# A two-block transformer on one core: gate banks, order of the mixers' last gates, and a split value product

## What is computed

```python
uv, c_q, c_kv, k_rope, z, xbc, dt_raw, gates = jnp.split(h @ w_in[l], IN_OFFSETS, axis=-1)
y_a = gmlp_mixer(uv, ...)                    # spatial gating
y_b = mla_mixer(c_q, c_kv, k_rope, ...)      # causal attention, 8 heads of 96
y_c = ssd_mixer(z, xbc, dt_raw, ...)         # state-space scan, 2 chunks of 128
g = jax.nn.sigmoid(gates).reshape(bsz, s, N_BRANCH, D_MODEL)
merged = (g[:, :, 0] * (y_a @ w_branch[l, 0])
          + g[:, :, 1] * (y_b @ w_branch[l, 1])
          + g[:, :, 2] * (y_c @ w_branch[l, 2]))
x = x + merged @ w_out[l]
```

## Time and profile before

| | |
|---|---|
| median of 3 runs | 3313.93 us (3313.74 to 3315.62) |
| profiled execution | 3314.97 us, its span 3313.2 us |
| PE busy | 3198.2 us, 97% |
| PEld busy | 2727.8 us, 82% |
| DVE busy | 1944.1 us, 59% |
| ACT busy | 1294.7 us, 39% |
| mean granted clock of TensorE | 0.987 of 2.4 GHz |
| chain that ended last | PE 89%, DVE 5%, issue 2%, ACT 2% |
| fp32 value product, L953 | 96 records, 41.8 us busy |

### The profile page before, as it was taken

How to read it: one execution, slowest core, us unless ns; L and a number is a source line. 1 busy time by engine, 2 the same in 40 slices (tenths; PEclk the granted TensorE clock), 3 DMA queues, 4 the chain that set the end, 5 groups by cost and what they waited for, 6 DMA issues and landing times.

```text
span 3313.2 us, 42938 instructions
## 1 busy us (share of the span) xinstructions
PE 3198.2 (97%) x17262; PEld 2727.8 (82%) x17262; DVE 1944.1 (59%) x2685; ACT 1294.7 (39%) x1785; POOL 103.3 (3%) x144
## 2 busy tenths in 40 slices
PE   8999889999998899999999999999999999999898
PEld 8988779899887799788877777778887888887797
DVE  6868568867686577674243344577334753345655
ACT  5446444444464454422223322232223222245543
POOL 1000000000000000000000000000000000022000
PEclk9999999999998999999999999999999999999999
DMA  7754347767553376553323222145333533253354
GB/s 242 243 188 166 112 139 258 248 210 235 177 171 122 127 237 224 174 179 109 114 90 101 77 89 77 64 163 168 99 111 108 188 130 105 99 134 89 98 183 153
DMA packets 334911, 496.96 MB, mean 150 GB/s; under 512 B 11042, under 2 KB 221884, under 8 KB 334716
## 3 DMA queue, kind: packets, MB, share of 16 engines
q1 hardware_dynamic: 330652, 483.46, 43.9%
q0 software_dynamic: 4064, 10.77, 1.5%
HBM read 493.09 MB, written 1.10 MB: 149 GB/s over the span
## 4 chain that ended last, share of the span: by engine, by line
PE 89%; DVE 5%; issue 2%; ACT 2%; POOL 1%; DMA 0%; DVEq 0%; POOLq 0%; ACTq 0%
PE bank L531 28%; PE bank L532 28%; PE bank L533 28%; DVE wlo L1550 1%; PE bank L953 1%; ACT whi L1090 1%; PE bank L661 1%; PE bank L544 1%; PE bank L676 0%; PE bank L938 0%; POOL small L2357 0%; POOL small L2362 0%; DVE bank L2294 0%; DVE small L2290 0%; ACT npr L1498 0%
## 5 line engine op out<-in xcount | busy, mean ns | idle before, releaser
L1550 DVE TENSOR_TENSOR wlo<-raw,whi 128x1024 fp32r<-128x1024 f32 (+1 forms) x780 | 933.9, 1211 | 995.6 <-ACT whi L1090 993.7
L1090 ACT ACTIVATE whi<-raw 128x1024 fp32r<-128x1024 f32 (+1 forms) x780 | 813.5, 1049 | 1189.8 <-PE bank L533 1186.9
L531 PE MATMUL bank<-xTh,whi 128*128 128x256 f32 (+1 forms) x3200 | 1045.5, 327 | 6.1 <-DVE xTl L1606 6.0
L533 PE MATMUL bank<-xTh,wlo 128*128 128x256 f32 (+1 forms) x3200 | 1039.4, 325 | 0.0
L532 PE MATMUL bank<-xTl,whi 128*128 128x256 f32 (+1 forms) x3200 | 1039.3, 325 | 0.0
L531 PEld LDWEIGHTS bank<-xTh,whi 128*128 128x128 f32 x3200 | 610.6, 191 | 68.7 <-issue 19.7
L533 PEld LDWEIGHTS bank<-xTh,wlo 128*128 128x128 f32 x3200 | 610.3, 191 | 49.1
L532 PEld LDWEIGHTS bank<-xTl,whi 128*128 128x128 f32 x3200 | 610.7, 191 | 48.3 <-issue 0.5
L531 PE MATMUL bank<-whi,hh 128*128 128x512 f32 x968 | 377.6, 390 | 0.0
L533 PE MATMUL bank<-whi,hl 128*128 128x512 f32 x968 | 376.7, 389 | 0.0
L532 PE MATMUL bank<-wlo,hh 128*128 128x512 f32 x968 | 376.6, 389 | 0.0
(11 more groups left out here) (337 smaller groups left out, 2318.4 us busy)
## 6 DMA issues: line engine op xcount, KB each, us to landing
raw<-in_ffn_w_in_dram SPq DMA_DIRECT2D x176, 1024.0 KB, 5.4
raw<-in_ffn_w_out_dram SPq DMA_DIRECT2D x80, 1024.0 KB, 5.0
mraw<-in_w_mod_dram SPq DMA_DIRECT2D x72, 1024.0 KB, 5.1
raw<-in_w_in_dram SPq DMA_DIRECT2D x44, 1024.0 KB, 5.1
raw<-in_ret_w_in_dram SPq DMA_DIRECT2D x24, 1024.0 KB, 5.1
raw<-in_w_branch_dram SPq DMA_DIRECT2D x12, 1024.0 KB, 5.0
raw<-in_nat_w_qkv_dram SPq DMA_DIRECT2D x12, 1024.0 KB, 5.1
raw<-in_ffn_w_out_dram SPq DMA_DIRECT2D x16, 512.0 KB, 3.6
```

The lines of the kernel that those rows point to most:

```text
L531: pe.matmul(ps, lh, rh, start=start, stop=False, skip_group_check=True)
L533: return pe.matmul(ps, ll, rh, start=False, stop=stop, skip_group_check=True)
L1090: nc.scalar.activation(hi, src, ACT.Copy).then_inc(*e.inc("hi", key, part))
L1550: nc.vector.tensor_tensor(lo, src, hi.bitcast(F32), ALU.subtract).then_inc(*e.inc("lo", key, part))
```

## The change

What it does, in four parts.

1. The rings: `SHORT` becomes banks 0 to 3, `LONG` 4 to 7. The units of the mixers of block one that came from `ALL` behind the first state of the scan now come from one of the smaller rings: branches, the turned outputs b and c, the second chunk's products and the output projection from `SHORT`, its sums from banks 6, 7, 4 and 5, the turned merged rows from `LONG`.
2. The order of TensorE and of the slabs: gate (2,1) is one slab half before and one behind `branch(1,0)`, with the turned outputs between its parts; then branches (2,0), (1,1), the first merged rows turned, branch (2,1). The other engines follow.
3. ScalarE and VectorE: the sigmoids of gate (1,1), the fourth projection, stand behind the last exponential in step 8 of the attention; in a step, turned pieces are copied before the split and the exponentials come behind it on ScalarE, and the maxima before it on VectorE. `heads_scaled` is divided into the sum and the scaling with other work between, `heads_rotated(1)` goes from before `turned_y(a)` to before `merge(0,0)`, `scan_decays(1)` before `scan_rows(0)`.
4. The value product of the retention: values and weighted scores are split into `rvh`, `rvl`, `rah` and `ral` and multiplied by `mm3`. The gate's rows `gbm` move to the place of `WX` and `wtmp`, and are loaded once head 3's weighted scores stand.

```diff
-SHORT, LONG = (0, 1, 2, 3, 4), (5, 6, 7)
-ALL, SCORES, TURNED, VALUES, UPPER = tuple(range(8)), (0, 1, 2, 3), (4, 5), (6, 7), (4, 5, 6, 7)
+SHORT, LONG = (0, 1, 2, 3), (4, 5, 6, 7)
+ALL, TURNED, VALUES = tuple(range(8)), (4, 5), (6, 7)
...
         gate(0, 1)
-        branch(0)
+        branch(0, 0)
+        branch(0, 1)
         gate(1, 0)
         gate(1, 1)
         gate(2, 0)
-        branch(1)
-        gate(2, 1)
-        branch(2)
+        c = GATES + 2 * D + 512
+        s.add((("g", l, 2, 1), 0), rows(m, 0, 4, c, 512), 4, 512)
+        branch(1, 0)
+        s.add((("g", l, 2, 1), 1), rows(m, 4, 4, c, 512), 4, 512)
+        branch(2, 0)
+        branch(1, 1)
+        branch(2, 1)
         for half in range(2):
             for n in range(2):
...
@@ -866,28 +879,32 @@
                 branch(0, 0, ytT[1])
                 scan_sums(1)
                 branch(0, 1, ytT[1])
-                gate(1, 0, lambda part: (head_turned(0) if part == 1 else attention(part - 2) if part > 1 else None))
+                gate(1, 0, -2)
                 scan_inside(1)
                 pe.wait_ge(*e.at("st", l))
-                ps = new("yo", l)
+                ps = new("yo", l, ring=SHORT)
...
-                gate(2, 0, lambda part: attention(6 + part))
-                turn_y(("b", l), yb, 4, 256, ("yb", l))
-                turn_y(("c", l), z, 4, 256, ("yc", l))
+                gate(1, 1, 2)
+                gate(2, 0, 6)
+                g21 = gate_banks(2, 1)
+                gate_part(2, 1, g21, 0)
+                turn_y(("b", l), yb, 4, 256, ("yb", l), SHORT)
+                gate_part(2, 1, g21, 1)
+                turn_y(("c", l), z, 4, 256, ("yc", l), SHORT)
                 pe.wait_ge(*e.at("yT", ("b", l), 1))
-                for n in range(2):
-                    branch(1, n, ytT[1])
-                gate(2, 1)
+                branch(1, 0, ytT[1])
+                gate_part(2, 1, g21, 2)
+                gate_part(2, 1, g21, 3)
                 pe.wait_ge(*e.at("yT", ("c", l), 3))
                 branch(2, 0, ytT[0])
+                branch(1, 1, ytT[1])
 
                 def merged_turned(n):
                     for u in range(2 * n, 2 * n + 2):
-                        ps = new("ty", ("m", l), u)
+                        ps = new("ty", ("m", l), u, ring=LONG)
                         for j in range(2):
                             for t in range(2):
                                 pe.wait_ge(*e.at("mg", l, n, t))
...
-                rows_by(("b", l, 2, 1), ("bp", l, 2, 1), b2, *ytT[0], 0, 4, (0,))
                 merged_turned(0)
-                rows_by(("b", l, 2, 1), ("bp", l, 2, 1), b2, *ytT[0], 2, 4, (1,))
+                branch(2, 1, ytT[0])
                 pe.wait_ge(*e.at("yT", ("m", l), 1))
                 wo = {}
                 for n in range(2):
-                    wo[n] = {t: new("wop", l, n, t) for t in range(2)}
+                    wo[n] = {t: new("wop", l, n, t, ring=SHORT) for t in range(2)}
                     rows_by((("wo", l, n), 0), ("wop", l, n), wo[n], *xT[256], 0, 8)
                     if n == 0:
                         merged_turned(1)
...
                     m.then_inc(*e.inc("rap", h, 1 + jt))
 
             def retained(h):
-                pe.wait_ge(*e.at("ra", h, 2))
-                pe.wait_ge(*e.at("rv", h, 3))
+                pe.wait_ge(*e.at("ral", h, 2))
+                pe.wait_ge(*e.at("rvl", h, 3))
                 for t in range(4):
                     ps = new("rop", h, t)
                     if t < 2:
-                        pairs = [(ra[:, 0, 256 * jt + t * P:256 * jt + (t + 1) * P], jt) for jt in range(2)]
-                        pairs += [(ra[:, 1 + jt, t * P:(t + 1) * P], 2 + jt) for jt in range(2)]
+                        pairs = [(0, 256 * jt, jt) for jt in range(2)] + [(1 + jt, 0, 2 + jt) for jt in range(2)]
                     else:
-                        pairs = [(ra[:, 1 + jt, t * P:(t + 1) * P], 2 + jt) for jt in range(2)]
-                    for i, (a, j) in enumerate(pairs):
-                        m = pe.matmul(ps[:, :], a, rv[:, j, :], start=i == 0, stop=i == len(pairs) - 1)
+                        pairs = [(1 + jt, 0, 2 + jt) for jt in range(2)]
+                    for i, (u, c, j) in enumerate(pairs):
+                        cols_of = slice(c + t * P, c + (t + 1) * P)
+                        m = mm3(ps[:, :], rah[:, u, cols_of], ral[:, u, cols_of], rvh[:, j, :], rvl[:, j, :],
+                                i == 0, i == len(pairs) - 1)
                     m.then_inc(*e.inc("rop", h, t))
 
...
@@ -1334,7 +1349,8 @@
                         if h >= 2:
                             act.wait_ge(*e.at("op", l, h - 2))
                         A(pT[h % 2][:, :], unit("ptp", l, h)[:, 0:384], ACT.Copy).then_inc(*e.inc("pT", l, h, frees=("ptp", l, h)))
-                    if i < HEADS:
+                    after(key, part)
+                    if 0 <= i < HEADS:
                         h = i
                         act.wait_ge(*e.at("nmax", l, h))
                         if h >= 2:
@@ -1346,9 +1362,9 @@
                               bias=small[:, o + 3:o + 4], accum_out=small[:, o + 5:o + 6])
                         m.then_inc(*e.inc("pr", l, h, frees=("sc", l, h)))
 
-                ahead(until, (("g", l, 0, 0), 0))
...
@@ -1359,26 +1375,38 @@
                 for n in range(2):
                     ahead(until, ("b", l, 0, n))
                 scan_exps(1)
-                gate(1, 0, lambda part: (head_turned(0) if part == 1 else attention(part - 2) if part > 1 else None))
+                gate(1, 0, -2)
                 sigmoids(1, 0)
-                gate(1, 1, lambda part: attention(2 + part))
-                sigmoids(1, 1)
-                gate(2, 0, lambda part: attention(6 + part))
+                gate(1, 1, 2)
+                for part in range(4):
+                    attention(6 + part, (("g", l, 2, 0), part // 2), part % 2)
+                    if part == 2:
+                        sigmoids(1, 1)
                 sigmoids(2, 0)
+                after((("g", l, 2, 1), 0), 0)
                 turned_y(("b", l), 4, 256, ytT[1][0])
+                after((("g", l, 2, 1), 0), 1)
                 turned_y(("c", l), 4, 256, ytT[0][0], lambda c: col(0, SSN + 4 * l + c))
-                for n in range(2):
-                    ahead(until, ("b", l, 1, n))
-                gate(2, 1)
+                for part in range(2):
+                    after(("b", l, 1, 0), part)
+                for part in range(2):
+                    after((("g", l, 2, 1), 1), part)
                 sigmoids(2, 1)
-                for n in range(2):
-                    ahead(until, ("b", l, 2, n))
+                for part in range(2):
+                    after(("b", l, 2, 0), part)
+                for part in range(2):
+                    after(("b", l, 1, 1), part)
+
+                def merged_turned(n):
                     for u in range(2 * n, 2 * n + 2):
                         act.wait_ge(*e.at("ty", ("m", l), u))
                         A(xT[256][0][:, 2 * u:2 * u + 2, :], unit("ty", ("m", l), u)[:, :]
                           .rearrange("p (j t) -> p j t", t=256), ACT.Copy).then_inc(*e.inc("yh", ("m", l), u))
-                    if n == 0:
-                        after(("b", l, 2, 1), 1)
+
+                merged_turned(0)
+                for part in range(2):
+                    after(("b", l, 2, 1), part)
+                merged_turned(1)
                 for n in range(2):
                     after((("wo", l, n), 0), 1)
                 after((("wo", l, 0), 1), 0)
...
+                    act.wait_ge(*e.at("ra", h, u))
+                    A(rah[:, u, :], ra[:, u, :], ACT.Copy).then_inc(*e.inc("rah", h, u))
                 if h == 1:
                     first_rows(0)
                 if h:
...
@@ -1997,6 +2034,8 @@
                         V.tensor_reduce(small[:, o:o + 1], ps[:, 0:P], AX, ALU.max)
                         link(V.tensor_reduce(small[:, o + 1:o + 2], ps[:, 256:512], AX, ALU.max))
                         TS(small[:, o + 2:o + 4], small[:, o:o + 2], -QK ** -0.5, None, ALU.mult).then_inc(*e.inc("nmax", l, h))
+                    if i < HEADS + 1:
+                        after(key, part)
                     if 2 <= i < HEADS + 2:
                         h = i - 2
                         o = 112 + 8 * (h % 2)
@@ -2010,10 +2049,12 @@
                         o = 112 + 8 * (h % 2)
...
@@ -2041,50 +2082,54 @@
                 ahead(until, ("kv", l))
                 dve.wait_ge(*e.at("kvp", l, 1, 1))
                 scan_decays(0)
-                ahead(until, (("uv", l, 1), 0))
+                after((("uv", l, 1), 0), 0)
+                heads_summed(0)
+                after((("uv", l, 1), 0), 1)
                 heads_scaled(0)
                 ahead(until, (("uv", l, 1), 1))
-                heads_rotated(0)
+                heads_rotated(0, lambda: after((("uv", l, 1), 1), 1))
```

(45 more changed lines are left out.)

110 lines of the change are left out of this document (62 added, 48 removed).

## The result

The changed kernel takes 3236.92 us, median of 4 runs (3233.21 to 3237.75), the kernel before 3314.53 us in the same comparison: a ratio of 0.9763, 95% interval 0.9747 to 0.9780. That is 77.6 us less. I had forecast 69.1 us less and 3245 us, with 3238 us as the low end: the time lies 1.1 us under the range. In the profiled executions the span went from 3313.2 to 3235.0 us, by 78.2 us.

The account below looks back on a forecast made before the run. TensorE bounds the kernel; its idle and slow-clock time in block one's mixers can go. Mixers 64.6 - 5.0 = 59.6, value product 8.5, key-copy wait 1.0: 69.1 us off 3314.97, median 3245 us; own range 3239 to 3255, eight-in-ten 3238 to 3264.

Parts of the forecast that it names:

- the charge: Both mixers of block one: 2.5 us a mixer held back for late banks and a tight place missing with clock drop.
- The clock term: Both mixers of block one: time lost at TensorE's lower clock comes back, about 9.8 us a mixer, 19.6 us.
- (1): Ahead of the gates, VectorE works while waiting for GpSimd's roots; TensorE's waits for low weight halves go, 1.2 us a mixer.
- (2): At `branch(0,0)`, rotating the second tile's heads later removes the 3.1 us wait; gate (1,0) finds its banks 0.6 us late.
- (3): Four gate banks remove waits at diagonal product (5.7, 4.5 us), gate (2,0) (4.7), attention turns (3.0); last gate waits 0.2 us.
- (4): ScalarE's two fewer table loads of 1.28 us a mixer are on no path: 0; without cover 1.3 us each.
- (5): Attention step on four banks instead of five: cost 0, ScalarE's exponentials having 1.2 us to spare.
- (6): Mixer tail: split last gate and interleaved branches remove waits of 1.7, 1.9 and 2.5 us; tightest merges spare 0.4, 0.3.
- A: VectorE replaces the waits as bound, gate (1,0) and merges late: 12 to 20 us more, say 3260 us; chance 0.22.
- B: Mixers' gates are not freed, sigmoids stay in the path: only 21 us gained, 3293 us; chance 0.05.
- C: Many short waits keep TensorE at 1.2 GHz from `branch(0,0)` to the last merge: 3365 us; chance 0.04.
- D: Both mixers: none of the 2.5 us a mixer held back is lost, 3240 us; chance 0.04.

## Why the prediction was wrong, and where it was right

**The idle time** was right: 43.3 us against 43.4 us, and even the charge in its place, 0.5 us at gate (1,0) in both mixers where I had 0.6 us. The mechanism (gates that hold banks, VectorE late, merges too close) is what the profile shows.

**The clock term, with the charge in it, is the step that failed:** 16.2 us forecast, 23.9 us less busy time measured. The 7.7 us are three things. First, 3.4 us of charge: a tight place in each mixer that would miss and draw a fall of the clock. No such fall came; the changed mixers have one, at the start of the first, and the kernel before has it too. Second, the price of the slowed stretches: I had 9.8 us a mixer, 19.6 us, from pairs of equal work of which one is shown; the stretches themselves give 21.0 us, 1.4 us more. Two waits, of 4.46 and 4.69 us, were followed in the second mixer by 6.8 us at 1.2 GHz each, and two in the first, of 5.71 and 2.99 us; the one pair of which I showed the rows lies in a stretch of 3.4 us. Third, a term that the sum did not have: 2.9 us of busy time that went with the waits and is no clock. The trace of before could have given the second: busy time in the stretches with a granted clock of 0.50, halved. The Trainium skill (TensorE: Matmul & The Clock Gate, HAM oscillation — how this bites in real kernels) reckons so, extra time as half of the time at 1.2 GHz. The two mixers agree: by that rule the clock gave back 21.0 us, the 19 waits fewer at 0.16 us each make 3.0 us, and the 24.0 us together stand against 23.9 us measured. A rougher way, the granted clock times the window, gives 0.05 x 279.90 + 0.04 x 279.24 = 25 us before and 0.01 x 246.87 = 2.5 us after, and counts idle time at the low clock as well.

**The range** let the low end go to 3238 us, "no charge and a little more clock". With its own bound, 12 us a mixer and no charge, it would have reached 3245 - 5.0 - 4.4 = 3235.6 us; it would have been right by luck in part, as that bound counts idle time and the 2.9 us are none of the clock's. Its other side was wide for a rival that did not come (VectorE the bound, 0.22).

**Outside the mixers** I had 9.5 us, it was 11.0 us. Between the releases at 1731.87 and 2164.33 us before, 1663.48 and 2087.29 us after, the stage of the value product took 432.46 and 423.81 us: 8.65 us against my 8.5 us. The wait for the key copy is gone (1.0 us). The other 1.3 us have no cause that I can name: they are within the 6 us by which the same work differed between kernels.

**By parts.** (1) and (2): I gave the rotation 3.1 us and the roots 1.2 us a mixer. With the rotation alone undone 0.4 and 0.6 us of the wait are back, with the roots as well 1.6 and 1.7 us, with ScalarE's scan exponentials too 3.0 and 3.2 us: three edits share what I gave to one, so the attribution was wrong though the sum was right. The roots' own 1.2 us a mixer were right (2.4 us in both). (3): the gates' waits went, and with the banks alone. The late sigmoids, on which I had the last gate depend, and (4), the two loads fewer, are worth nothing: right for the loads; the last gate doesn't need the late place. (5): cost 0, right, but my 1.2 us to spare held for the old order of the step; in the new one even 3.65 us more of ScalarE (two loads and the sigmoids) fit. (6): the waits in my list are 1.7 + 2.5 us in the first mixer and 1.7 + 1.9 + 2.5 us in the second, 10.3 us, to which comes the clock behind them; the tail is worth 13.4 to 14.7 us. Both tight merges held. (What I expected of the run with the old tail counts the 1.9 us in both mixers, which is one too many.)

**Rivals.** A did not come: VectorE had room at the turned columns (1.49 us idle) and the gate waited 0.5 us. B did not: the run with banks alone excludes it. C did not: the changed mixers have 8 waits and a granted clock of 0.99 and 1.00, and nine short waits in a feed-forward left the clock alone; whether a denser row would bring C about is open. D, no charge at all, was the nearest, at 3240 us: of the 4.1 us that it lacked against the profiled executions the clock's price makes 1.4 us, the busy time of the waits 2.9 us and all outside the mixers 1.5 us, less 1.7 us of waits that stayed.

## What to carry to other kernels

Price the clock by the stretches in which it is granted at 0.50, half of TensorE's busy time in them, and not by a pair of rows. Busy time over equal instruction counts holds more than the clock: each wait adds a little to it. Where the sum names a bound, the range has to reach it. Judge an edit of a few microseconds between marks that both kernels share: the total moved by up to 6 us for the same work. Undo parts one at a time and add them one at a time as well, and compare the sums: here 7.9 us against 17.6 us, and most of the gap went with an edit that nobody had undone. Look for it in pairs of traces that differ in that edit alone up to the point in question.

## What the runs showed of the hardware

Single waits of TensorE of up to 1.5 us in a feed-forward, nine of them 12 us apart or alone, cost about their length (25 waits, 18.5 us, 19.3 us in the span) and left the granted clock at full. In the feed-forwards and the mixers of these kernels each wait of 2.76 us and more drew a fall to 1.2 GHz, which over six of them (2.96 to 9.06 us) cost about 2 us a wait beyond the length; between 1.8 and 2.8 us some did and some didn't. Behind a turn of normalised rows, where waits of 1.3 and 1.0 us follow each other closely, falls come and go from kernel to kernel, and part of their cost is hidden: with the clock at full TensorE waits up to 1.4 us for the turned columns instead (4.5 us in four waits in the kernel with the roots in place, 1.7 us in two in the changed one). Outside the mixers the former has 18 us less at 1.2 GHz, and its time there is 5.1 us shorter, not 9 us.
